# Norms, decay matrices and first products of the delta-rule mixer laid between the last chunks of the projection

## The reference, cut to what matters

```python
proj = h @ w_in                                   # 4096 columns beside 16 gate columns
conv = silu(conv4(q, k, v of A))                  # four taps along the tokens
qa = _l2norm(qa) * GDN_DK ** -0.5;  ka = _l2norm(ka)
G = jnp.cumsum(gc, axis=-1)                       # per chunk of tokens
decay = jnp.exp(G[:, None] - G[None, :])          # i >= j, else 0
a_low = (kb @ k.T) * decay                        # strictly lower, kb = k * beta
u = solve(I + a_low, vb);  w = solve(I + a_low, kb * exp(G))
attn = (q @ k.T) * decay
...
wts = jnp.exp(dl - mt[..., None]) * qki           # B: its own decay matrix times q k
```

## Time and profile before

| | us |
|---|---|
| runs, median (lowest to highest) | 984.24 (980.75 to 984.91) |
| the profiled execution | 976.55 |
| its span, first to last instruction | 974.8 |
| mean granted clock of TensorE in it | 0.963 |
| busy: TensorE, VectorE, ScalarE, GpSimd | 906.9, 397.8, 178.6, 218.1 |

### The profile page before, as it was taken

One profiled execution on the slowest core, in us unless ns is written; L12 is line 12 of the kernel. 1 busy time (PEld: TensorE's weight loads), 2 busy tenths in 40 slices (PEclk: granted clock), 3 DMA queues, 4 the chain that ended last, 5 costly groups with the idle time before them and its releaser, 6 DMA issues.

```text
span 974.8 us, 12310 instructions
## 1 busy us (share of the span) xinstructions
PE 906.9 (93%) x4952; PEld 489.0 (50%) x4952; DVE 397.8 (41%) x824; ACT 178.6 (18%) x316; POOL 218.1 (22%) x322
## 2 busy tenths in 40 slices
PE   8999997998998999899989979899889999999992
PEld 5888866885363433333333368744434333333330
DVE  4599508736635212222224279602552121211125
ACT  0411140323020111110101253301401111111111
POOL 4679992401020510100100111100202101110000
PEclk9999997999998999999999999999889999999997
DMA  9546729203869978999999936660499999999952
GB/s 273 113 161 243 265 111 301 95 12 107 276 213 406 370 295 355 403 417 401 410 401 424 421 124 195 213 274 0 180 391 358 403 406 403 396 409 408 411 244 89
DMA packets 83419, 277.27 MB, mean 284 GB/s; under 512 B 25240, under 2 KB 44134, under 8 KB 60694
## 3 DMA queue, kind: packets, MB, share of 16 engines
q1 hardware_dynamic: 70298, 255.86, 68.5%
q10 hardware_dynamic: 10660, 16.49, 5.3%
q0 software_dynamic: 2400, 4.07, 1.4%
HBM read 260.97 MB, written 18.01 MB: 286 GB/s over the span
## 4 chain that ended last, share of the span: by engine, by line
PE 81%; DVE 7%; DMA 7%; ACT 2%; issue 1%; POOL 0%; SPq 0%; DVEq 0%; ACTq 0%
PE ps L1846 22%; PE ps L342 12%; PE ps L1870 11%; PE ps L2526 6%; PE ps L1888 6%; PE ps L1793 4%; DMA x_rows<-work 3%; PE ps L799 3%; DMA ring<-in_moe_w_up 3%; PE ps L2388 1%; PE ps L305 1%; PE ps L1482 1%; PE ps L2403 1%; PE ps L1847 1%; PE ps L645 1%
## 5 line engine op out<-in xcount | busy, mean ns | idle before, releaser
L1846 PE MATMUL ps<-ring,work 128*64 128x512 f32 x416 | 189.9, 610 | 4.1 <-DMA ring<-in_moe_w_up 2.7
L1847 PE MATMUL ps<-ring,work 128*64 128x512 f32 x416 | 189.9, 610 | 0.0
L1930 DVE TENSOR_TENSOR work<-ps,work 64x512 f32<-64x512 f32 x32 | 33.7, 1054 | 208.7 <-ACT work L1901 208.7
L342 PE MATMUL ps<-work,ring 128*128 128x264 f32 x512 | 115.2, 387 | 0.0
L1846 PEld LDWEIGHTS ps<-ring,work 128*64 128x64 f32 x416 | 56.0, 140 | 115.8 <-issue 109.3
L1870 PE MATMUL ps<-ring,work 128*64 128x512 f32 x216 | 100.1, 607 | 6.3 <-issue 4.9
L342 PEld LDWEIGHTS ps<-work,ring 128*128 128x128 f32 x512 | 96.8, 190 | 16.4
L1871 PE MATMUL ps<-ring,work 128*64 128x512 f32 x216 | 100.2, 607 | 0.0
L1251 POOL TENSOR_TENSOR ring<-ring 128x512 f32<-128x512 f32 (+5 forms) x76 | 90.4, 1207 | 9.5 <-DVE ring L1247 6.2
L1940 DVE COPY work<-ps 64x512 f32<-64x512 f32 x32 | 22.2, 694 | 156.5 <-PE ps L1871 156.5
L1951 POOL COPY work<-work 64x1 int32<-64x1 int32 x30 | 6.1, 203 | 314.6 <-PE ps L1793 277.1
(11 more groups left out here) (488 smaller groups left out, 1252.0 us busy)
## 6 DMA issues: line engine op xcount, KB each, us to landing
ring<-in_moe_w_down SPq DMA_DIRECT2D x27, 2048.0 KB, 19.4
ring<-in_moe_w_gate SPq DMA_DIRECT2D x52, 1024.0 KB, 12.8
ring<-in_moe_w_up SPq DMA_DIRECT2D x52, 1024.0 KB, 14.7
ring<-in_w_in ACTq DMA_DIRECT2D x6, 2048.0 KB, 9.1
work<-in_moe_w_gate SPq DMA_DIRECT2D x12, 1024.0 KB, 17.0
work<-in_moe_w_up SPq DMA_DIRECT2D x12, 1024.0 KB, 19.2
work<-in_moe_w_down SPq DMA_DIRECT2D x5, 2048.0 KB, 25.8
s_out_mats<-ring SPq DMA_DIRECT2D x4, 1280.0 KB, 4.8
```

The source lines that it names most:

```text
L342: last = nc.tensor.matmul(ps[:, proj_bank(j), 0:T], win[g % 2][:, k, (j % 4) * P:(j % 4 + 1) * P], xT[:, k], start=k == 0, stop=k == DC - 1)
L1846: nc.tensor.matmul(ps[0:SLOT, 5, :], xgT[s][:, c], gate_w[slot][:, c], start=c == 0, stop=c == DC - 1)
L1847: last = nc.tensor.matmul(ps[SLOT:P, 5, :], xgT[s][:, c], up_w[slot][:, c], start=c == 0, stop=c == DC - 1)
L1930: nc.vector.tensor_tensor(hid[s][0:SLOT].rearrange("t (c p) -> t p c", c=4), strided(ps[SLOT:P, 5, :]), strided(sg[s][SLOT:P]), ALU.mult). ...
```

## The change

The projection takes three banks for chunks 0 to 27 and two for 28 to 31; a chunk waits for the last chunk that used its bank. The work named below is issued by TensorE ahead of the chunk given: G spread at 24, square sums of q and k and beta spread at 25, roots of k spread at 27, k k at 28, roots of q spread at 29, q k and B's decay rows at 30. The square sums take 8 matmuls instead of 32 (each head's row in the quadrant that reads it), here and at the outputs. Silu and squares of q and k move from chunk 26 to 22 and 23 on ScalarE, silu of v goes behind chunk 31; ScalarE takes the exponents of both decay matrices (as a Relu with a bias from `pos_cols`, then an exponential with scale -1) from VectorE. VectorE makes `pos_cols` before chunk 8, multiplies the decay by beta first (`gate_b`), then by the upper triangle, and does norms, level 0 and `at_f` in the projection. The k transposes come behind the projection, the v transposes in levels 1 and 2. GpSimd makes level 1 without waiting for chunk 31.

```diff
         def proj_bank(j):
-            return 1 + j % 4
+            return 1 + j % 3 if j < 28 else 1 + (j + 1) % 2
...
-                if j >= 4:
-                    t.wait_ge(*ac.at(f"proj{j - 4}"))
+                if proj_before(j) is not None:
+                    t.wait_ge(*ac.at(f"proj{proj_before(j)}"))
...
+                if j == 24:
+                    gdn_pe_gates(t)
+                if j == 25:
+                    gdn_pe_squares(t)
+                if j == 27:
+                    gdn_pe_norm(t, range(4, 8), (0, 6, 7, 5))
+                if j == 28:
+                    gdn_pe_kk(t)
+                if j == 29:
+                    gdn_pe_norm(t, range(0, 4), (0, 6, 7, 3))
+                if j == 30:
+                    gdn_pe_qk(t)
+                    ml_pe_decay(t)
...
-                if j == 26:
+                if j == 22:
                     a.wait_ge(*dv.at("conv"))
-                    nc.scalar.activation(cv, cv, ACT.Silu).then_inc(*ac.done("silu_cv"))
-                    a.wait_ge(*ac.last())
-                    a.wait_ge(*dv.at("conv_rest"))
+                    nc.scalar.activation(cv[:, 0:8], cv[:, 0:8], ACT.Silu).then_inc(*ac.done("silu_qk"))
+                if j == 23:
+                    a.wait_ge(*ac.at("silu_qk"))
+                    a.wait_ge(*pe.at("new_rows"))
                     nc.scalar.activation(sq, cv[:, 0:8], ACT.Square).then_inc(*ac.done("sq_cv"))
+                    gdn_act_gates(a)
+                if j == 24:
+                    gdn_act_roots(a)
+                if j == 30:
+                    ml_act_decay(a)
+            nc.scalar.activation(cv[:, 8:12], cv[:, 8:12], ACT.Silu).then_inc(*ac.done("silu_v"))
+            a.wait_ge(*ac.at("proj31"))
...
+                    v.wait_ge(*dv.last())
+                    for i, col in enumerate((NEG_G, I_F)):
+                        nc.vector.tensor_scalar(pos_cols[:, i], cols[:, col], -1.0, None, ALU.mult).then_inc(*dv.done("pos_cols"))
...
+        def squares_pe(halves):
+
+            for half in halves:
+                for r in range(4):
+                    h = 4 * half + r
+                    last = nc.tensor.matmul(ps[quad(r), 0, 0:T], head_col(h, 32), sq[:, h], start=half == 0, stop=half == 1)
+            return last
+
+        def gdn_pe_gates(t):
+
+            t.wait_ge(*dv.at("conv_rest"))
+            for h in range(H):
+                last = nc.tensor.matmul(ps[:, 6 + h // 2, (h % 2) * SEQ:(h % 2 + 1) * SEQ], row_of(h), R[0:H, RT_, 0:SEQ],
+                                        start=True, stop=True)
+            last.then_inc(*pe.done("G_all"))
...
+        def mix_pe(t):
+            t.wait_ge(*ac.at("proj30"))
+            gdn_pe_tokens(t, 0, 4, "k_tok")
+            t.wait_ge(*dv.at("attn_low"))
+            gdn_pe_tokens(t, 1, 4, "k_tok")
+            t.wait_ge(*ac.at("proj31"))
...
-            for h in range(8):
-                if h % 4 == 0:
-                    t.wait_ge(*ac.at(f"sq_o{h // 4}"))
-                for r in range(4):
-                    last = nc.tensor.matmul(ps[quad(r), 0, 0:T], head_col(h, 32), sq[:, h], start=h == 0, stop=h == 7)
+            for half in range(2):
+                t.wait_ge(*ac.at(f"sq_o{half}"))
+                last = squares_pe((half,))
...
+            v.wait_ge(*dv.at("conv"))
+            v.wait_ge(*ac.at("gate"))
+            v.wait_ge(*pe.at("beta_all"))
+            nc.vector.tensor_tensor(flat(gate_b), banks(4, 2), flat(gate), ALU.mult).then_inc(*dv.done("gate_b"))
+            v.wait_ge(*dv.at("gate_b"))
+            nc.vector.tensor_tensor(gate, gate, upper.unsqueeze(1).to_broadcast([P, 8, P]), ALU.mult).then_inc(*dv.done("gate_low"))
...
+            for h in range(H, 8):
+                normed(h, "k_norm")
+            v.wait_ge(*pe.at("proj27"))
+            for i in range(TT):
+                nc.vector.tensor_tensor(tinvT[:, rows[i]], gate_b[:, rows[i]], level[:, 0].unsqueeze(1).to_broadcast([P, H, P]), ALU.mult).then_inc(*dv.done("level0"))
...
         def mix_pool(pool):
-            pool.wait_ge(*pe.at("proj31"))
+            pool.wait_ge(*dv.at("levels"))
             for b in range(1, 7):
...
+                if b == 2:
+                    pool.wait_ge(*pe.at("proj31"))
```

More of the change, by code:

```diff
@@ new lines, in gdn_pe_gates, with gdn_pe_squares @@
+        def gdn_pe_gates(t):
[4 more added lines that the diff above has]
+            last.then_inc(*pe.done("G_all"))
+        def gdn_pe_squares(t):
+            t.wait_ge(*ac.at("sq_cv"))
+            squares_pe((0, 1)).then_inc(*pe.done("ss"))
+            for h in range(H):
+                for i in range(TT):
+                    last = nc.tensor.matmul(bank4(4 + i)[:, h], row_of(h), R[0:H, RB_, i * P:(i + 1) * P], start=True, stop=True)
+            last.then_inc(*pe.done("beta_all"))
@@ new lines, in gdn_pe_norm, with gdn_pe_kk @@
+        def gdn_pe_norm(t, heads, at):
+            if heads[0] == 4:
+                t.wait_ge(*ac.at("qdec"))
+                t.wait_ge(*dv.at("gate_b"))
+            else:
+                t.wait_ge(*dv.at("k_norm"))
+                t.wait_ge(*ac.at("proj26"))
+            for h in heads:
+                nc.tensor.matmul(ps[:, at[h % 4], 0:T], quad_row_of(h % 4, h), R[quad(h % 4), RA], start=True, stop=True).then_inc(*pe.done(f"rn{h}"))
+        def gdn_pe_kk(t):
+            t.wait_ge(*dv.at("k_norm"))
@@ L556, in mix_pe, with gdn_pe_qk @@
                     last = nc.tensor.matmul(bank4(4 + i)[:, h], k, k, start=True, stop=True)
[L557 to L562 removed]
+                last.then_inc(*pe.done(f"kk{i}"))
+        def gdn_pe_qk(t):
+            t.wait_ge(*dv.at("qk_norm"))
@@ L570, in mix_pe, with gdn_pe_values @@
-            last.then_inc(*pe.done("qk"))
-            between = (ml_pe_decay, lambda t: ml_pe_kv(t, 0), lambda t: ml_pe_kv(t, 1), lambda t: ml_pe_qk(t, 0),
-                       lambda t: ml_pe_qk(t, 2), ml_pe_state, ml_pe_num)
-            for b in range(7):
+                last = nc.tensor.transpose(bank4(2 + i)[:, h], cv[:, first + h, i * P:(i + 1) * P], ident)
+            last.then_inc(*pe.done(f"{name}{i}"))
+        def gdn_pe_values(t, i):
+            t.wait_ge(*ac.at("silu_v"))
+            t.wait_ge(*dv.at(f"k_tok{i}"))
+            gdn_pe_tokens(t, i, 8, "v_tok")
@@ L884, in mix_dve @@
+            v.wait_ge(*pe.at("proj31"))
+            for i in range(TT):
+                v.wait_ge(*pe.at(f"qk{i}"))
+                nc.vector.tensor_tensor(attnT[:, rows[i]], bank4(3 * i), gate[:, rows[i]], ALU.mult).then_inc(*dv.done("attn_low"))
             nc.vector.memset(kqb, 0.0).then_inc(*dv.done("kqb_zero"))
-            for h in range(8):
-                v.wait_ge(*pe.at(f"rn{h}"))
-                nc.vector.scalar_tensor_tensor(cv[:, h], cv[:, h], QSCALE if h < H else 1.0, ps[:, h, 0:T], ALU.mult, ALU.mult).then_inc(*dv.done("qk_norm"))
@@ L929, in mix_dve @@
+            for b in range(1, 7):
+                for i in range(TT):
                     mine = slice(4 * i, 4 * i + 4)
```

163 lines of the change are left out of this document (72 added, 91 removed).

## The result

The changed kernel took 977.2 us (median of 6 runs, 975.95 to 980.63), the kernel before 984.6 beside it (6 runs, 980.75 to 986.27). The ratio is 0.9936, 95% interval 0.9917 to 0.9956: 6.3 us faster by the ratio, 7.4 by the medians. 975.2 was predicted.

The account below looks back on a forecast made before the run. TensorE was taken as the bound, with a broken chain of waits behind the projection; 10.0 + 1.4 - 2.4 = 9.0 us gained made 976.55 into 967.5 profiled, plus the 7.7 us offset 975.2 us, range 969.5 to 982.

Parts of the forecast that it names:

- (a): Projection chunk 3, with three banks, waits for ScalarE to empty chunk 0's bank: 3.2 us lost.
- (b): Two VectorE sign flips before chunk 8's convolution make TensorE's G product wait ahead of chunk 24: 1.6 us lost (0.3 to 2.5).
- (c): Work inserted between projection chunks on TensorE lengthens the projection by 13.0 us.
- (d): ScalarE and VectorE finish the inserted work's inputs in time during the projection, with 2 us slack at tight places: no cost.
- (e): Behind the projection, level 1 starts at 158.6, VectorE's queue sets its first subtraction, and level 2 starts 10.0 us earlier.
- (f): Square sums of the outputs, a quarter of the TensorE time, let the output norms end earlier: 1.4 us gained.
- (g): The clock falls once after the new wait at chunk 3, one cold stretch: 2.4 us lost.
- Rival B: No clock fall in the wait at 29 us, and cheap sign flips: 12.6 us gained, 971.6 us; chance 0.17.
- Rival D: The clock falls at each insertion and the early wait, seven places at 2.5 us: 990.3 us; chance 0.05.
- "Loads and matmuls move together and the gain stays": Expert weight loads start only behind the mixer's last steps, so the 9.0 us gain persists through the expert stage.
- Rival E: The gain is given back because expert weights set the pace from a transfer that doesn't move: 983.5 us; chance 0.08.
- The constant offset: The profiled execution of before lies 7.7 us under the runs' median, added to the forecast 967.5 to give 975.2.

Follow-up runs that it names:

- e3: The kernel before with only the new bank rule (three banks, two from chunk 28): 988.09 us, ratio 1.0049.
- e6: The changed kernel with four banks for chunks 0 to 19, VectorE's small steps ahead of chunk 31, ScalarE's tanh behind level 1's copies: 968.09 us, 0.9847.
- e7: The kernel before, unchanged, run and profiled a second time: 982.95 us, ratio 0.9996.
- e5: The changed kernel with VectorE's memset, small copies, q product and mLSTM keys moved into its idle time before chunk 31: 975.09 us, ratio 0.9908.
- e1: The changed kernel with four banks again for chunks 0 to 19, three only from chunk 20: 972.02 us, ratio 0.9884.
- e2: The changed kernel with three filler matmuls (six passes of 512 columns) on TensorE ahead of chunk 3: 975.37 us, ratio 0.9921.
- e12: The changed kernel with 48 small matmuls (96 passes) in TensorE's wait for layer 0's first expert lists: 973.16 us, ratio 0.9904.
- e4: The kernel before with only the shorter square sums, 8 matmuls instead of 32 at both places: 986.83 us, ratio 1.0031.
- e8: e4 with TensorE's first three filler matmuls cut into 51 of 32 columns, restoring the instruction count of before: 1001.05 us, ratio 1.018.
- e10: e6 with 48 small filler matmuls in TensorE's wait for layer 0's first expert lists: 967.59 us, ratio 0.9842.

## Why the prediction was right, point by point

- **(a), three banks.** 3.2 us predicted, 2.99 measured, in e3 and in after alike. Right.
- **(b), the sign flips ahead of G.** 1.6 us predicted (0.3 to 2.5), 0.1 measured: the copy for G ends at 115.06 + 1.74 = 116.80, and G starts at 116.94 on the heels of chunk 23. The wait of (a) is no cover for it, as e6, without that wait, has 0.22 us ahead of G. The two flips took 1.00 us of VectorE, within what I allowed:

```profile
85.13 1.00 DVE L526 TENSOR_SCALAR work<-work 128x8 f32<-128x8 f32 x2
```

but the copy ended 91.4 us behind the start of chunk 0 in before (109.64 - 18.23) and 91.6 in e6 (111.66 - 20.07). The convolution's first step behind the flips made up for them: it took 0.34 us in after and in e6, where the same step took 1.16 in before. After, then before:

```profile
86.04 0.34 DVE L529 TENSOR_SCALAR work<-work 128x256 f32<-128x256 f32 x1
```

```profile
78.04 1.16 DVE L501 TENSOR_SCALAR work<-work 128x256 f32<-128x256 f32 x1
```

The failed step is that a step added to VectorE delays by its own length: beside GpSimd the next step came out 0.8 us shorter. Why it did is not shown. Mis-sized, outside its bounds.

- **(c), the insertions.** 13.0 us predicted. In e6, with neither wait nor fall of the clock, the projection is 132.97 - 120.0 = 12.97 us longer. Right.
- **(d), ScalarE and VectorE keep up.** Right: no idle time before the k k products or the q k products. The prices held for the most part. In after level 0's two masks, with both inputs in SBUF, took 1.19 us each beside GpSimd (0.65 to 1.75 allowed); the two subtractions L996 took 0.75 and 1.08, where I had some 0.7. The Trainium skill, SBUF — State Buffer, section Who interferes with whom, says that a step with two SBUF inputs contends with GpSimd and a step with at most one does not, unless it is of a kind (copies and steps with a scalar among them) that can take the shared ports too. The 0.69 us of the product that reads PSUM, with GpSimd busy all through it (0.75 of 0.75 us), agrees with it:

```profile
137.44 2.37 DVE L986 TENSOR_TENSOR ring<-work,const 128x512 f32<-128x512 f32 x2 [2.33 <-PE ps L361]
139.84 0.69 DVE L990 TENSOR_TENSOR ring<-ps,ring 128x512 f32<-128x512 f32 x1
```

  The prediction told that rule without its exception. The convolution's steps with a scalar have one SBUF input and do pay here, in before: 1.16 to 1.42 us beside GpSimd's long run, 0.35 to 0.40 at 46 to 52 us, ahead of it.
- **(e), the joint.** End of the projection to level 2: 10.0 us predicted, 9.36 measured. Right, down to which queue sets it (first subtraction at 166.06 for 164.6, on a projection that ends 2.2 later). "From there the levels repeat what they did" failed by 1.2 us: from level 2 to level 6 after takes 25.60 us (193.14 - 167.54), before 24.41 (200.45 - 176.04). The two masks of B's decay matrix took 1.27 us before, with GpSimd idle for most of that time; now they run beside it, 2.35 us for both, and TensorE waits 0.46 us ahead of level 4:

```profile
174.80 2.35 DVE L1036 TENSOR_TENSOR work<-work,const 128x512 f32<-128x512 f32 x2
...
178.56 1.16 PE L697 MATMUL ps<-ring 128*128 128x128 f32 x8 [0.46 <-DVE ring L962]
```

- **(f), the output square sums.** 1.4 us predicted. From the last residual product to the next layer's first product over the outputs pass 245.72 - 231.97 = 13.75 us in e7 and 234.35 - 222.41 = 11.94 in after; 0.46 of it is that product itself, which ran at lower clock in e7 (1.81 for 1.35). So 1.35 us are gained there. Right, for TensorE's path; its price comes 320 us later (below).
- **(g), the clock.** One cold stretch predicted at 2.4 us; it came, and cost 1.7 (12.63 for 10.95). Rival B, no fall, didn't come in this profile; its first half, the wait without a fall, did in e5. Rival D, a fall at each insertion, is out: 1.00 in 108 to 158 us of after, past all six. But at G it may fall: it did in four of the eight profiles with G there (e1, e2, e5, e12), 1.7 us each. D's reason, thin work with four rows of weights, has something to it (last section). The second fall, at 219.6 us, is in the kernel before as well (e7).
- **The sum.** 9.0 us predicted up to the first expert load, 8.9 measured against the profile the sum was made on. That agreement is partly luck: (a), (b), (e) and (g) came out 3.0 us better in total (level 2 starts 147.2 us behind chunk 0, for 166.0 + 2.4 - 18.23 = 150.2), and the levels (1.2) and the fall at 219 us (1.6), which that profile was spared, took it back.
- **"Loads and matmuls move together and the gain stays".** This step failed. Behind the first load, 2.7 us or so went to the last combine (e4, e8, e12). Rival E named giving back, but by the pace of the weights; that is not what happened at the combine. Another 0.5 to 2 us go between the first load and the first gate and up product: 30.4 to 31.1 us in all nine kernels with the shorter square sums and the count not made up before the load, 28.3, 28.3, 28.4 and 29.9 in the four others. They sit in the landing of the token rows behind the first weight loads: the copy that waits for them starts 27.7 to 28.2 us behind the first load in the nine, 26.0, 26.0, 26.1 and 27.0 us in the four. The rest is lower clock in the transposes behind it. This part is nearer to rival E. I have no experiment on why the rows land later, and e7, the kernel before, has half of it.
- **The constant offset.** The profiled execution was taken as 7.7 us under the median for both kernels. For after it was 0.04 us off. So the profiled execution of after, forecast at 967.5, took 9.7 us more, and the offset of 7.7 took nearly all of that out again. The first profile of before was short by chance: against e7, 2.1 us in the start (1.7 of them in a product that ran at lower clock in e7, 5.49 us for 3.80), 1.5 between level 2 and the first expert load, 1.5 up to the first gate and up product, the rest behind.

So the forecast lies 2.0 us under the result. The mechanism in the front held; the return behind the first load, 4.0 us against e7 and 6.0 against the first profile, wasn't foreseen, and that the total still came out near is luck: the offset of 7.7 covered it.

## What to carry to other kernels

Put short dependent steps into the gaps between dense matmuls only as far as their producers are early there, and look at the resource that the move takes away: here the fourth bank, which the inserted work (the spread of beta, ahead of chunk 25) needs only late in the projection and which was given up for all of it, cost 4.8 us, and two lines returned them. Work taken from a path has a second effect by its instructions: compare the stages behind the change too, against a second profile of the kernel before. A sum made on one profile should be told as distances between events, with a second execution for their scatter.

## What was not expected of the hardware

- **A wait that goes by the count of instructions.** 3.4 to 3.8 us without a releaser ahead of one combine, in all six kernels with 96 passes fewer (90 in e2) and in that with 48 fewer, in none of the six profiles with the full count, some 250 us or more behind the place where passes were added or removed.
- **The price of a small matmul is in its form, and in its place.** 128x32 weights with 8 columns, four side by side: 0.99 us for 96, 10 ns a pass. 128x128 weights with 16 columns at full clock, in e7: 116 ns a pass.

```profile
290.01 3.72 PE L1534 MATMUL ps<-fix,work 128*128 128x16 f32 x32 [0.51 <-ACT work L1521]
```

  128x128 weights with 32 columns at the start of the kernel (e8): 215 ns a pass. There all work is slow: six passes of 512 columns take 5.37 us in after, 0.9 us each, where two take 1.02 later on, 0.5 each.
- **Small copies within SBUF can pay for GpSimd, though they have one input.** With 32 columns, L1004 took 0.31 us in after and the same copy 1.30 in e5, beside a run of GpSimd's tensor steps:

```profile
145.78 8.47 POOL L1337 TENSOR_TENSOR ring<-ring 128x640 f32<-128x640 f32 x5
...
151.36 1.30 DVE L1001 COPY work<-work 128x32 f32<-128x32 f32 x1
```

- **The clock can fall with TensorE busy.** Behind G, after 0.15 us of waiting, it fell in e1, and not in the profile of after, with the same instructions in the same order there (below). Between 100 us and the output norms the 13 profiles have twelve falls with TensorE at work and no wait over 0.16 us just before. All stand 0.03 to 1.1 us behind the end of a group of passes with four rows of weights: four behind G, seven behind a group of G's form ahead of the residual products (e7, after, e1, e2, e8, e10, e12), one behind the spread of beta (e3). But such a group doesn't always bring a fall: none came behind B's decay rows at chunk 30, of G's form too, in any of the eight profiles that have them there. No experiment took the groups away. Behind the output norms the clock falls in other work as well.

```profile
116.00:118.00 2.00, 2.00 (x6) 1.51 (x5) 0.00 (x0) 1.93 (x8) 2.00 (x2) 0.50 1.05 344
```
